# The last layer's modulation vector: from TensorE in the first block to VectorE in the first feed-forward block

## The reference, cut to what matters

```python
# first block, one layer
mod = (s_lat @ w_ada[l] + b_ada[l]).reshape(B, N_MOD, 1, D)      # s_lat = silu(c)
mod_c = (s_ctx @ w_ada[l] + b_ada[l]).reshape(N_MOD, 1, 1, D)
# second block, two layers
for l in range(DEPTH_2):
    ctx_out = l < DEPTH_2 - 1
    sh_a, sc_a, g_a, sh_f, sc_f, g_f = jnp.split(silu_c @ mod_w[l] + mod_b[l], 6, axis=-1)
    csh_a, csc_a, cg_a, csh_f, csc_f, cg_f = jnp.split(silu_cc @ mod_w[l] + mod_b[l], 6, axis=-1)
    a_lat = modulate_2(h_lat, sh_a, sc_a)
    a_ctx = modulate_2(h_ctx, csh_a, csc_a)
    ...                                                          # attention
    h_lat = h_lat + g_a * o_lat
    h_lat = h_lat + g_f * swiglu(modulate_2(h_lat, sh_f, sc_f), ffn_w_gate_up[l], ffn_w_down[l])
    if ctx_out:
        ...                                                      # the same for the context
return rms_norm_2(h_lat, final_norm)
```

## Time and profile before

| | us |
|---|---|
| median of 3 runs | 2271.17 (2270.33 to 2273.9) |
| span of the profiled execution | 2266.1 |
| TensorE busy | 2166.4 (96%) |
| VectorE busy | 1060.0 (47%) |
| ScalarE busy | 474.8 (21%) |
| bytes loaded | 430.6 MB, mean 190 GB/s |
| products of the modulation with tiles of matrices two and three (`ring,sw`) | 50.0 (x384) |

### The profile page before, as it was taken

The page is one execution under the profiler, slowest core; times in us unless marked ns, Lnnn a source line. Parts: engine busy times, 40 slices in busy tenths (PEclk is TensorE's granted clock), DMA queues, the critical chain, the costliest instruction groups (busy, mean ns, idle before and its releaser), DMA issues.

```text
span 2266.1 us, 39462 instructions
## 1 busy us (share of the span) xinstructions
PE 2166.4 (96%) x16246; PEld 1505.8 (66%) x16246; DVE 1060.0 (47%) x2304; ACT 474.8 (21%) x1071; POOL 0.2 (0%) x4
## 2 busy tenths in 40 slices
PE   6999999999999999999999999989999999999998
PEld 4554456898885333333334577468888887779998
DVE  2046777545414222222223567254544643647785
ACT  4010342444212000000012137211111001441110
POOL 0000000000000000000000000000000000000000
PEclk9999999999998999999999999999999999999999
DMA  9275888000456999999991120112222222123442
GB/s 374 96 274 225 337 352 333 22 4 4 162 196 239 376 422 422 422 422 422 422 417 68 56 93 2 54 59 93 76 92 93 84 103 105 64 73 134 168 168 75
DMA packets 59621, 430.64 MB, mean 190 GB/s; under 512 B 6608, under 2 KB 6864, under 8 KB 8016
## 3 DMA queue, kind: packets, MB, share of 16 engines
q1 hardware_dynamic: 57600, 416.31, 46.5%
q10 hardware_dynamic: 1872, 12.17, 1.4%
HBM read 427.40 MB, written 1.05 MB: 189 GB/s over the span
## 4 chain that ended last, share of the span: by engine, by line
PE 81%; DMA 10%; DVE 7%; ACT 1%; issue 1%; SPq 0%; ACTq 0%; DVEq 0%
PE bank L627 78%; DMA arena<-in_w 8%; DMA ring<-in_w 1%; PE bank L806 1%; DVE bank L2019 1%; DVE arena L2040 1%; DVE normed L1975 0%; DMA arena<-in_xin 0%; DVE arena L2238 0%; PE bank L1107 0%; PE bank L1121 0%; PE bank L671 0%; DVE arena L2243 0%; DVE arena L2279 0%; DVE arena L2295 0%
## 5 line engine op out<-in xcount | busy, mean ns | idle before, releaser
L627 PE MATMUL bank<-arena 64*64 64x64 f32 (+9 forms) x8950 | 867.7, 298 | 21.4 <-DMA arena<-in_w 6.2
L627 PEld LDWEIGHTS bank<-arena 64*64 64x64 f32 (+4 forms) x8950 | 622.6, 153 | 233.7 <-issue 185.0
L627 PE MATMUL bank<-normed,ring 128*128 128x256 f32 (+3 forms) x1984 | 506.5, 413 | 11.5 <-DVE normed L1994 5.9
L627 PEld LDWEIGHTS bank<-normed,ring 128*128 128x128 f32 (+1 forms) x1984 | 350.2, 192 | 156.0 <-issue 114.0
L627 PE MATMUL bank<-ring,arena 128*64 128x512 f32 (+1 forms) x1000 | 208.1, 600 | 11.1 <-DMA ring<-in_w 9.6
L627 PE MATMUL bank<-arena,ring 128*128 128x256 f32 (+1 forms) x1136 | 214.8, 339 | 4.1 <-DVE arena L2747 3.6
L627 PEld LDWEIGHTS bank<-arena,ring 128*128 128x128 f32 x1136 | 184.2, 191 | 22.7 <-DVE arena L2747 4.2
L627 PEld LDWEIGHTS bank<-ring,arena 128*64 128x64 f32 (+1 forms) x1000 | 62.6, 132 | 142.1 <-issue 112.2
L2527 DVE TENSOR_TENSOR arena<-arena,bank 128x512 f32<-128x512 f32 x68 | 46.6, 685 | 131.0 <-PE bank L627 129.1
L1882 ACT ACTIVATE arena<-arena 128x256 f32<-128x256 f32 (+1 forms) x88 | 32.0, 363 | 344.0 <-DVE arena L2744 217.6
L627 PE MATMUL bank<-normed,arena 128*128 128x256 f32 (+2 forms) x424 | 83.6, 340 | 0.0
(11 more groups left out here) (393 smaller groups left out, 1759.6 us busy)
## 6 DMA issues: line engine op xcount, KB each, us to landing
ring<-in_w SPq DMA_DIRECT2D x297, 1024.0 KB, 8.3
arena<-in_w SPq DMA_DIRECT2D x97, 1024.0 KB, 17.6
arena<-in_xin ACTq DMA_DIRECT2D x1, 2048.0 KB, 9.0
arena<-in_nab ACTq DMA_DIRECT2D x1, 2048.0 KB, 8.6
con<-in_con ACTq DMA_DIRECT2D x1, 1280.5 KB, 14.5
sw<-in_sw ACTq DMA_DIRECT2D x1, 1280.0 KB, 8.5
sw<-in_sw ACTq DMA_DIRECT2D x1, 1168.0 KB, 19.3
arena<-in_xin ACTq DMA_DIRECT2D x1, 1024.0 KB, 5.4
```

Source lines behind the costliest of these rows:

```text
L627: return nc.tensor.matmul(o, l, r, start=start, stop=stop, **kw)
```

## The change

The third matrix leaves the first block and `MODS` becomes 48. Its 24 tiles are packed in another way: a row of an output channel, 1024 inputs long, lies along the columns, so that a tile holds two rows of outputs for each of 128 partitions. They are put among the 34 weight tiles of f0 (`FFN_TILES`). VectorE multiplies a row with the silu of the condition, held on all partitions in `cond_rows`, and sums it in the same instruction (`tensor_tensor_reduce`, 128 x 1024, into one column of `mod2b`, with the bias as the start value): 16 outputs for context and latent, 32 for the latent alone, 64 instructions. 50 of them stand behind L2747's counterpart (L2807), two or three per gate/up tile, 14 in the down tiles. The product without the sum goes into the tile itself for the latent, into spare room (`products`) for the context. SyncE waits for the counter `modulated` where it loads over a modulation tile. ScalarE loads the condition rows (`crow`, 1 MB) after the even attention and applies silu to them, two instructions of 128 x 1024. VectorE waits for `modulated` at the start of the down part and before n5, and clears `mod2b` at the start. The counters of single norms are merged into one for all norms.

In the first block a round has two modulation tiles instead of three, the attention 10 instead of 18, the norm 4 as before, the decay 2 instead of 6, the merge 8 instead of 12, all behind pair 3. Six slabs are turned round instead of nine.

```diff
-PRE = (3 * N_ADA + N_QKVP + N_RW + N_MERGE + N_OUT) // UPT
-POST = (N_EVEN + N_OUT + N_FFN + N_ODD + N_OUT + N_FFN) // UPT
+PRE = (2 * N_ADA + N_QKVP + N_RW + N_MERGE + N_OUT) // UPT
+POST = (N_EVEN + N_OUT + N_FFN + N_ODD + N_OUT + N_FFN + N_ADA) // UPT
 ADA = N_ADA // UPT
...
-MODS = 3 * ADA
-
-IN_ROUND = 3
-WITH_DIFF, WITH_NORM, WITH_LORA = (0, 2, 2, 2, 2, 2, 2, 2, 2, 1, 1), (1, 1, 1, 1), (1, 1, 1, 0, 1, 1, 1, 0)
+MODS = 2 * ADA
+
...
+OUTS_BOTH, OUTS = 2 * KD, 6 * KD
+LAYER_MODS = [(o, x) for o in range(OUTS_BOTH) for x in (1, 0)] + [(o, 0) for o in range(OUTS_BOTH, OUTS)]
+WITH_DOWN = 14
...
+def layer_mods(m):
...
+    n = len(LAYER_MODS) - WITH_DOWN
+    return [i for i in range(len(LAYER_MODS)) if m == (i * (FT - 1) // n if i < n else FT + len(DOWN) + (i - n) // 2)]
+
+FFN_TILES = {"f0": [], "f1": [("weights", m) for m in range(FT + KD // 2 * len(DOWN))]}
+for _, _m in FFN_TILES["f1"]:
+    FFN_TILES["f0"].append(("weights", _m))
+    FFN_TILES["f0"] += [("mods", LAYER_MODS[i][0] // 2) for i in layer_mods(_m)
+                        if i == min(y for y, z in enumerate(LAYER_MODS) if z[0] // 2 == LAYER_MODS[i][0] // 2)]
+MOD_DONE = {j: 1 + max(i for i, z in enumerate(LAYER_MODS) if z[0] // 2 == j) for j in range(OUTS // 2)}
...
+IN_ROUND = 2
+WITH_DIFF, WITH_NORM, WITH_LORA = (0, 1, 1, 1, 1, 1, 1, 1, 1, 1, 1), (1, 1, 1, 1), (1, 0, 0, 0, 1, 0, 0, 0)
...
-BEHIND = [("pairs", range(0, 2)), ("mods", LEFT[:-KD]), ("pairs", range(2, 4)), ("mods", LEFT[-KD:]), ("pairs", range(4, 6))]
+BEHIND = [("pairs", range(0, 4)), ("mods", LEFT), ("pairs", range(4, 6))]
...
+        cond_rows = [sw[:, 0:D], sw[:, D:2 * D]]
+        products = region(FT * T, D)
...
+            def ffn_tile(name):
+
+                while FFN_TILES[name][st["unit"] // UPT - marks["tile_" + name]][0] == "mods":
+                    st["unit"] += UPT
+                    st["free"].append(None)
+                return unit(UPT)
+
...
-                    if i in (3, 7):
-                        modulation(LEFT[-KD - 1] if i == 3 else LEFT[-1])
+                    if i == 7:
+                        modulation(LEFT[-1])
...
+            act.dma_start(sw[:, 0:2 * D], dram["crow"]).then_inc(S("cond_rows_in"), 16)
+            act.wait_ge(S("cond_rows_in"), 16)
+            for x in range(2):
+                f(cond_rows[x], cond_rows[x], ACT.Silu).then_inc(S("cond_rows_silu"), 1)
...
+            v.does(V.memset(mod2b[:, :], 0.0))
...
+            def layer_modulations(m):
+
+                for i in layer_mods(m):
+                    o, x = LAYER_MODS[i]
+                    t = marks["tile_f0"] + FFN_TILES["f0"].index(("mods", o // 2))
+                    dve.wait_ge(S("cond_rows_silu"), 2)
+                    dve.wait_ge(ring_full[t % RING], 16 * (t // RING + 1))
+                    w = ring[:, t % RING * TILE + o % 2 * D:t % RING * TILE + (o % 2 + 1) * D]
+                    if x and i >= 2:
+                        dve.wait_ge(S("modulated"), i - 1)
+                    V.tensor_tensor_reduce(out=products if x else w, in0=w, in1=cond_rows[x], scale=1.0,
+                                           scalar=Q("mod_b1", 2 * o + x), op0=MUL, op1=ADD,
+                                           accum_out=mod2b[:, 2 * o + x:2 * o + x + 1]).then_inc(S("modulated"), 1)
...
+            dve.wait_ge(S("modulated"), len(LAYER_MODS))
...
-                        sp.wait_ge(full, tile_free[t - RING])
+                        if tile_free[t - RING] is None:
+                            kind, j = FFN_TILES["f0"][t - RING - marks["tile_f0"]]
+                            sp.wait_ge(S("modulated"), MOD_DONE[j])
+                        else:
+                            sp.wait_ge(full, tile_free[t - RING])
```

More of the change, by code:

```diff
@@ L2872, in pack @@
     gated = lambda m, n: [gate_u[n][m], br_u[n][m]]
-    mods = np.concatenate([slabs(z) for z in (g["w_ada"][0], g["mod_w_2"][0], g["mod_w_2"][1])])
+    mods = np.concatenate([slabs(z) for z in (g["w_ada"][0], g["mod_w_2"][0])])
     mods = mods.reshape(MODS, UPT, P, P)
@@ L2898, in ffn @@
                 out.append(tile.reshape(UPT, P, P))
-        return out
+        out = [np.concatenate(out[2 * f:2 * f + 2]) for f in range(FT)] + out[2 * FT:]
+        last = g["mod_w_2"][1].reshape(KD, P, OUTS // 2, 2, P).transpose(2, 3, 0, 4, 1).reshape(OUTS // 2, UPT, P, P)
+        return [out[x] if kind == "weights" else last[x] for kind, x in FFN_TILES[f"f{l}"]]
     ev = g["even_w_in_2"][0]
@@ L2949, in pack @@
             "cnt": np.concatenate([con["cnt"], rows(g["lambda_qk"])], 1), "swa": con["swa"],
-            "fin": rows(g["final_norm_2"]), "sw1": sw1, "sw2": sw2, "xin": xin, "xin2": xin2, "nab": nab}
+            "fin": rows(g["final_norm_2"]), "crow": np.concatenate([rows(g["c_2"]), rows(g["c_ctx_2"])], 1), "sw1": sw1, "sw2": sw2, "xin": xin, "xin2": xin2, "nab": nab}
 def program(nc, arrays):
```

34 lines of the change are left out of this document (22 added, 12 removed).

## The result

The changed kernel takes **2246.7 us** (median of 4 runs, 2243.0 to 2248.7) against 2271.7 of the kernel before beside it: a ratio of 0.9886, 95% interval 0.9874 to 0.9898, or 25 us. The forecast was 2245.8. Its profiled execution spans 2243.8 us.

A forecast was written before the change was run, and what follows sets the result against it. TensorE was taken to bound the kernel, 81% of the span. 7.9 + 5.9 + 12.1 - 0.5 = 25.4 us off 2266.1 gives a span of 2240.7, plus 5.1 to the median: 2245.8 us, own range 2243 to 2248.5.

The forecast's parts named there:

- Rounds, 7.9: Rounds, eight tiles less: seven at 0.86 us give 6.0, slabs 1.9; sum 7.9 us (6.0 to 9.0).
- the eighth tile that gave nothing: Rounds: one of eight removed tiles gains nothing, since TensorE there already waits 0.83 us for VectorE's L2132.
- The slabs: Rounds: two turned slabs with a wait become one, with or without; 1.4 to 2.2 us saved, taken as 1.9.
- Attention, 5.9: Attention, eight tiles less: seven give 6.0 us, a slab 0.5, less 0.6 for the softmax; 5.9 (5.3 to 6.5).
- Decay and merge, 12.1: Decay and merge, eight tiles less: the scan starts at 389.2 instead of 401.29; 12.1 us (10.9 to 13.4).
- Start of the merge: End of the decay: TensorE starts the merge at 310.6 instead of 317.99, or 308 at full clock.
- VectorE going on behind its own chain: Into the merge: VectorE no longer idles for L1725 and goes on at 311.7 instead of 317.55, 5.9 us earlier.
- f0, 0.5: f0: 64 reductions of 1.2 to 1.5 us fit VectorE's idle time; cost 0.5 us (0 to 4).
- the slower rival: f0: `tensor_tensor_reduce` might take 6.7 us each, making the kernel 180 us slower, 2400; chance 0.06.
- More comes back: Rival, 2241 us: decay at full clock, loads ready for the run of eight, f0 loses nothing; 30.5 us gained; chance 0.16.
- Less comes back: Rival, 2251 us: rounds 6.0, attention 5.3, merge late by one more cold start, 0.5 to 2 lost in f0; chance 0.20.
- a scan later than 379 us: Sign of being wrong: the scan was forecast to start 26 us earlier, at 375.5 instead of 401.3.

The follow-up runs named there:

- after_again: The changed kernel once more, nothing altered, beside runs of the kernel before on the same chip: 2247.1 us, ratio 0.9883.
- skip_rounds: Kernel before, one of three modulation tiles in each of the eight rounds cut to one small product, still loaded: 2266.5 us, ratio 0.9972.
- work_kept: Changed kernel with TensorE's work as before: 24 tiles' products run again, only the 24 loads gone: 2288.4 us; up to the scan 13.3 us under before.
- skip_attention: Kernel before, one modulation tile in each of the attention's steps 1 to 8 cut to one small product, still loaded: 2273.3 us, ratio 1.0003.
- sums_twice: Changed kernel with each of the 50 reductions of f0's gate/up tiles run twice: 2250.8 us.
- no_f0: Changed kernel without the third matrix: no 24 tiles, 64 reductions, condition rows or two silu: 2249.0 us, ratio 0.9889.
- spread: Changed kernel with the merge's eight modulation tiles put four behind pair 1 and four behind pair 3: 2243.5 us, ratio 0.9868.

## Why the prediction was right, and where it was not

**The sum** was 25.4 us, the runs gave 25.0 (27.0 beside after_again), and the profiles 24.4 less 0.5 from the rounds on. That 2245.8 came within 1 us of 2246.7 is partly luck. The span was forecast at 2240.7 and came out at 2243.8, 3.1 us longer; the 5.1 us added to get from the span to the median came out at 2.9. Every run's time stands 1.8 us above its span. The other 3.3 of the 5.1 said that the profiled execution of the kernel before was quicker than its median, by things that change from execution to execution: it started at 121.1 us and had the pair behind the run of eight at the full clock.

**Rounds, 7.9:** 8.7. The mechanism held: skip_rounds shows the tiles at 5.7, and TensorE's wait for L2132 grew from 0.83 to 1.70 us, the eighth tile that gave nothing. The slabs were sized a little low: two with a wait became one without, 2.7 us in work_kept instead of 1.9.

**Attention, 5.9:** 5.65, for a reason that is half of the true one. I costed it as TensorE's time only and took 0.6 off for the softmax. TensorE's time alone would have given nothing (skip_attention), and so would the loads alone (work_kept). The number came out because both go with the same tile. The row that said so was there: DMA at 0.99 beside TensorE at 38.06 of 38.30. It stood in the text as a fact about the stage and not as a second bound of the sum. For a change that moved the products and kept the loads, the same step would have been wrong by its whole size.

**Decay and merge, 12.1:** 10.1 in the first profile and 9.5 in the second. Start of the merge: forecast 310.6 - 288.9 (121.1 + 128.8 + 39.0) = 21.7 us after the attention's end, measured 20.8, so 7.4 of the 12.1 were forecast for the decay and 8.4 came. VectorE going on behind its own chain (5.9 us earlier): confirmed, L2237 waits for nothing. That TensorE's waits for loads ahead of 296.7 would go: confirmed, and work_kept shows that it was the loads (6.5 of 8.4 us). The merge is the mis-sized term: 4.7 forecast, 1.7 and 1.2 measured against the first profile. I had TensorE take 76.6 us from its start to its end; it took 378.55 - 3.05 - 296.94 = 78.6. The run of eight waited for loads as forecast and released VectorE late as forecast (1.46 us at L2262, in the 0 to 2.5), but the pair behind it ran at 1.2 GHz, 5.91 us for 3.62. In the kernel before's own profile that pair took 3.69, and I took it to stay so. In the executions here it took 5.5 to 6.2 us in six profiles, 4.4 in one and 3.7 in four, with the run of eight or its like ahead: it is likelier cold (at the lower clock) than warm, for before as for after. So the two profiles compare a warm merge with cold ones. Like with like the term holds: cold 86.0 and 86.5 (skip_rounds and skip_attention, whose merge is that of before) against 81.6 to 82.1, warm 83.3 against 79.4 (sums_twice), that is 3.9 to 4.9 us. The section of the Trainium skill that the prediction cites ("TensorE: Matmul & The Clock Gate", "HAM oscillation — how this bites in real kernels") speaks for it; I applied it to the decay, and there the trace agrees that work behind a wait runs slow (behind the wait of 2.28 us a tile takes 1.93 us at 285.48, 1.07 at full clock), but it cost little: the merge began at the equal of 309.7, not at 311 or later. It should have been weighed at the run of eight.

**f0, 0.5:** none to 0.5. The estimate of 1.2 to 1.5 us came out at 1.21 from one to the next (1.28 for one alone). But the prediction read its best row wrongly. It says that `tensor_tensor_reduce` has no row in the trace of before, and takes L2019 for a neighbour that multiplies and sums. Line 2019 of the kernel before is a `tensor_tensor_reduce`, with add and minimum as its operations, and it ran there 48 times. So the rows at hand spoke against the slower rival more strongly than its 0.06 says. The threshold at which VectorE would pace f0, 2.5 us per reduction, was a little high: in sums_twice (2.4 us) VectorE already loses 0.36 us per tile. The point at which the gain is gone, 3.1 us, lies between the doubled (2.4 us, +4) and the tripled sums (3.6 us, +75), so the slower rival's mechanism exists and only its price was absent. The 0.5 and 0.8 us that the two profiles of the changed kernel lose behind the scan are not f0's: no_f0 has 1865.5 there as well.

**The rivals.** "More comes back" needed the merge without its run of eight; spread is that, at 2243.5, and it took a change of order to get it. "Less comes back" did not come: neither a late merge nor a cost in f0. One sign was badly chosen: a scan later than 379 us was to mean wrong, and it began at 378.55 in the first profile and at 381.75 in the second, of which 1.7 and 4.4 us were there before the rounds began. From the first product of the rounds on it is 24.4 and 23.9 us earlier, under the 26 of the forecast.

## What to carry to other kernels

Where two resources are both full in a stage, as in the attention here, the gain of taking work off is at most the smaller of the two reliefs, and an experiment that takes off one alone shows nothing: cost a moved tile once in the engine's time and once in the loads' time, and take the lower. Work that an idle engine can do in one fused instruction is free nearly up to the average of its idle time per period (11.9 of 12.07 us was already too much here), not up to the gap in which it stands. And after a move, look for the place where the freed engine now runs dry: a run longer than the ring, or a bank whose reader comes late in its own queue, was worth 3.6 and 11 us here, beside 6.5 for eight more tiles out of the rounds.

## What the runs showed of the hardware that was not expected

The same first instructions of this program take 120.5 to 125.5 us in the 14 profiles, in the order of TensorE's granted clock from 38 to 95 us: 120.5 to 121.1 us in the four with 1.00, 122.8 with 0.97, 124.3 to 125.5 in the nine with 0.93 to 0.95. That is 5 us, or a fifth of the effect measured here, and it lies in the execution and not in the kernel: a difference of two single profiles has to be taken from a common event on, not from zero.

TensorE's clock can stay at the lower level for the real work behind a few waits. With waits of 2.42 and 1.50 us among eight thin tiles the next 16 records took 5.91 us in place of 3.62; with waits of 0.47, 1.66, 1.38 and 1.74 us in sums_twice they took 3.69. What tells the two apart was not settled.
